# Layer ends, the first product cycle and head 17's projections of a two-layer encoder: squares in eight tiles, other orders, and readers on other engines

## The reference

```
layer 0: h = rmsnorm(x);  8 latent-attention heads + 8 differential heads  ->  x += concat(heads) @ w_out
         h = rmsnorm(x);  x += (silu(h @ w_gate) * (h @ w_up)) @ w_down            # w_gate, w_up: 1024 x 2816
layer 1: h = rmsnorm(x);  q, k, v, q_idx, k_idx, w_idx = split(h @ w_in)
         score = sum_heads(w_idx * relu(q_idx . k_idx));  keep the best keys of each query: 128 (prompt), 48 (sample)
         8 heads: softmax(q.k + bias, kept keys only) @ v   ->  x += concat(heads) @ w_out
         h = rmsnorm(x);  x += (silu(h @ w_gate) * (h @ w_up)) @ w_down
y = rmsnorm(x)
```

## Time and profile before

| | |
|---|---|
| median of 3 runs | 1752.54 us (1750.75 to 1753.04) |
| the profiled execution | 1750.98 us, span 1749.2 us |
| TensorE busy | 1683.5 us, 96% of the span |
| VectorE, ScalarE, Pool busy | 1114.9, 802.3, 598.0 us |
| mean granted clock of TensorE | 0.987 |

### The profile page before, as it was taken

One profiled execution on the slowest core, in us unless ns is written; L12 is line 12 of the kernel. 1 busy time (PEld: TensorE's weight loads), 2 busy tenths in 40 slices (PEclk: granted clock), 3 DMA queues, 4 the chain that ended last, 5 costly groups with the idle time before them and its releaser, 6 DMA issues.

```text
span 1749.2 us, 31768 instructions
## 1 busy us (share of the span) xinstructions
PE 1683.5 (96%) x12345; PEld 1622.6 (93%) x12345; DVE 1114.9 (64%) x2087; ACT 802.3 (46%) x1515; POOL 598.0 (34%) x455
## 2 busy tenths in 40 slices
PE   7999999999999899999999999799998999999998
PEld 6889998899898899999999999799988999999998
DVE  4666555645556697478477689533346974884776
ACT  4355545344546455145235444443355551452453
POOL 3344435454533322012102345464453220121022
PEclk9999999999999999999999999899999999999999
DMA  7121232322232124233323232332323232333231
GB/s 203 51 60 49 63 85 67 84 82 72 76 100 72 49 63 119 73 93 91 107 74 88 66 90 64 98 94 67 104 64 85 76 106 73 97 96 98 73 88 64
DMA packets 252105, 145.46 MB, mean 83 GB/s; under 512 B 21934, under 2 KB 242156, under 8 KB 251956
## 3 DMA queue, kind: packets, MB, share of 16 engines
q1 hardware_dynamic: 247080, 135.41, 27.3%
q0 software_dynamic: 4032, 7.77, 1.7%
q10 hardware_dynamic: 844, 0.24, 0.1%
HBM read 130.69 MB, written 15.32 MB: 83 GB/s over the span
## 4 chain that ended last, share of the span: by engine, by line
PE 82%; DVE 10%; ACT 4%; issue 2%; DMA 1%; POOL 1%; ACTq 0%; DVEq 0%; POOLq 0%
PE ACC L1191 40%; PE ACC L1551 7%; PE ACC L1553 7%; PE ACC L1552 7%; PE T L1191 3%; PE ACC L1446 2%; PE S L1191 2%; PE S L1421 2%; DVE SCO L2646 1%; DVE TOP L2643 1%; PE S L1553 1%; PE S L1551 1%; PE S L1552 1%; ACT PR L1976 1%; PE T L1434 1%
## 5 line engine op out<-in xcount | busy, mean ns | idle before, releaser
L1191 PE MATMUL ACC<-XGh,WH 128*128 128x288 f32 x1024 | 234.9, 311 | 9.2 <-DVE YK L2499 4.2
L3075 POOL TENSOR_TENSOR WL<-RAW,WH 128x1024 fp32r<-128x1024 f32 (+3 forms) x84 | 180.6, 2154 | 175.2 <-ACT WH L1851 174.8
L1191 PE MATMUL ACC<-XGl,WH 128*128 128x288 f32 x1024 | 222.1, 299 | 0.0
L1191 PE MATMUL ACC<-XGh,WL 128*128 128x288 f32 x1024 | 221.8, 299 | 0.0
L3224 POOL TENSOR_TENSOR HF<-SG,U 128x576 f32<-128x576 f32 x44 | 64.1, 1458 | 438.4 <-ACT SG L2111 411.7
L1851 ACT ACTIVATE WH<-RAW 128x1024 fp32r<-128x1024 f32 (+3 forms) x159 | 153.1, 971 | 81.9 <-PE ACC L1191 43.7
L1551 PE MATMUL ACC<-TB,WH 128*128 128x288 f32 x640 | 189.0, 295 | 0.6
L1553 PE MATMUL ACC<-TB,WL 128*128 128x288 f32 x640 | 188.8, 295 | 0.0
L1552 PE MATMUL ACC<-TB,WH 128*128 128x288 f32 x640 | 188.4, 294 | 0.0
L1191 PE MATMUL ACC<-HH,WH 128*128 128x288 f32 x1032 | 179.2, 295 | 0.0
L1191 PEld LDWEIGHTS ACC<-XGh,WH 128*128 128x128 f32 x1024 | 165.1, 192 | 15.0 <-DVE YK L2499 5.1
(11 more groups left out here) (427 smaller groups left out, 4361.6 us busy)
## 6 DMA issues: line engine op xcount, KB each, us to landing
RAW<-in_w_gate_dram SPq DMA_DIRECT2D x44, 512.0 KB, 3.9
RAW<-in_w_up_dram SPq DMA_DIRECT2D x44, 512.0 KB, 4.7
RAW<-in_w_down_dram SPq DMA_DIRECT2D x32, 512.0 KB, 4.0
RAW<-in_w_in_even_dram SPq DMA_DIRECT2D x29, 512.0 KB, 5.2
RAW<-in_w_in_odd_dram SPq DMA_DIRECT2D x28, 512.0 KB, 4.5
RAW<-in_w_out_even_dram SPq DMA_DIRECT2D x16, 512.0 KB, 4.2
RAW<-in_w_down_dram SPq DMA_DIRECT2D x16, 384.0 KB, 3.5
RAW<-in_w_out_odd_dram SPq DMA_DIRECT2D x8, 512.0 KB, 5.1
```

Of the source, the lines that this page charges most:

```text
L1191: ins = pe.matmul(out[0:m, 512 * b:512 * b + width], left, right[:, b * width:(b + 1) * width], start=(first and part == 0), stop=(last an ...
L3075: pool.tensor_tensor(WL[slot][:, 0:n], RAW[slot][:, 0:n], WH[slot][:, 0:n].bitcast(F32), ALU.subtract).then_inc(w_lo_pool, 1)
```

## The change

**Squares.** At norms 1 and 3 (the layers' attention ends) ScalarE writes the squares to eight tiles SQB and waits for nobody; VectorE adds them up in three wide additions at the start of `ffn`, in place of Pool's eight. **Output tiles.** Tile 7 of both bursts uses pair 1 and not 0. `first_half` runs the two products with MIXh first, waiting for job_hi, and the one with MIXl after it, waiting for job_lo; in layer 1 tiles 0 and 2 are begun before the weighted values of head 23, tiles 1 and 3 after them, and four tiles are halved in place of three. Head 23's last output tile is added to X before the turned probabilities of slot 5 are split.

**First cycle.** TensorE does all of u0 before the sum of squares, and three steps of g1 between the sum and its spreading. VectorE and ScalarE work the token sums, weight sums and gates in another order, and hidden_hi(0) moves up.

**Heads 16 and 17.** ScalarE reads q, k and v of head 17 from PSUM, Pool multiplies them by RSTD (y_made). ScalarE also takes KF and VF of head 16. VectorE's late selection is in one piece. Pool loads the cached keys of head 17 before head 16. Job v of head 16 is in slot 2, job k of head 17 in slot 4.

```
-    return 3 if h == 23 else 4
+    return {16: 2, 23: 3}.get(h, 4)
...
-    BURST_PAIRS = {14: (3, 0, 2, 1, 3, 0, 2, 0), 22: (1, 3, 0, 2, 1, 0, 2, 0)}
+    BURST_PAIRS = {14: (3, 0, 2, 1, 3, 0, 2, 1), 22: (1, 3, 0, 2, 1, 0, 2, 1)}
...
+            if norm in (1, 3):
+                return SQB[:, m, :]
...
+            def first_half(p, m, low):
+                out = pair(acc.at("wo", p, m)) if low else open_pair("wo", p, m)
+                wh, wl = unit_ready("wo", p, m // 4)
+                cols = slice((m % 4) * P, (m % 4 + 1) * P)
+                if low:
+                    pe.wait_ge(job_lo, jobs.made("o", p))
+                else:
+                    pe.wait_ge(job_hi, jobs.made("o", p))
+                for left in (wh,) if low else (wh, wl):
+                    for b in range(2):
+                        right = (MIXl if low else MIXh)[:, 0, b * HALF:(b + 1) * HALF]
+                        pe.matmul(out[:, 512 * b:512 * b + HALF], left[:, cols], right, start=(left is wh and not low), stop=False)
...
                     if kind_of(h) == "dsa":
-                        first_half(h - 1, 0)
+                        for low in (False, True):
+                            first_half(h - 1, 0, low)
+                            first_half(h - 1, 2, low)
...
                 plain("g", 0, 6, DT)
+                plain("u", 0, 3, DT)
                 norm_sum(norm)
-                plain("u", 0, 3, 6)
+                plain("g", 1, 0, 3)
                 norm_rows(norm)
-                plain("u", 0, 6, DT)
-                for m in range(1, PLAIN):
-                    plain("g", m, 0, DT)
-                    plain("u", m, 0, DT)
+                plain("g", 1, 3, DT)
+                plain("u", 1, 0, DT)
...
+                if kind_of(h) == "dsa":
+                    whole_first_half(3)
+                halved = 4 if kind_of(h) == "dsa" else 3
...
-                unread = n - 1 if norm == 0 else n
-                if unread > 0:
-                    act.wait_ge(sacc, unread)
+                if norm == 0 and n > 1:
+                    act.wait_ge(sacc, n - 1)
...
+                    if h == 16 and s == 1:
+                        take_first_values()
...
+            def take_projection(what):
+                before = {"q": ("v", 16), "k": ("q", 17), "v": ("k", 17)}[what]
+                dst = {"q": YQ[:, :], "k": raw_keys(17)[:, 0:NT], "v": raw_values(17)[:, 0:NT]}[what]
+                act.wait_ge(acc_done, acc.made(what, 17))
+                act.wait_ge(acc_free, acc.made(*before))
+                if what == "q":
+                    act.wait_ge(job_lo, jobs.made("q", 16))
+                act.activation(two(dst), halves(pair(acc.at(what, 17))), ACT.Copy,
+                               scale=DSA_SCALE / DIFF_SCALE if what == "q" else 1.0).then_inc(acc_free, 1)
...
+            take_projection("q")
             cached_keys_hi(16)
             begin("k", 17)
             job("q", 17)
+            take_first_keys()
             begin("v", 17)
+            take_projection("k")
+            take_projection("v")
...
-                    if s == 1:
+                    if s == 1 and h != 16:
                         take_values(h)
+                    if h == 23 and s == 5:
+                        evacuate(("wo", *out_tile(h, s)), add_to_x(out_tile(h, s)[1]))
...
+            def add_squares(norm):
+                dve.wait_ge(sq_done, XFIN * norm + DT)
+                link(dve.tensor_tensor(SQB[:, 0:4, :], SQB[:, 0:4, :], SQB[:, 4:8, :], ALU.add))
+                link(dve.tensor_tensor(SQB[:, 0:2, :], SQB[:, 0:2, :], SQB[:, 2:4, :], ALU.add))
+                dve.tensor_tensor(SACC[:, :], SQB[:, 0, :], SQB[:, 1, :], ALU.add).then_inc(sacc, XFIN)
...
                 begin("u", layer, 0)
+                evacuate(("u", layer, 0), lambda out: dve.tensor_copy(two(U[:, 0, :]), halves(out)))
                 token_sum(layer, 1)
-                evacuate(("u", layer, 0), lambda out: dve.tensor_copy(two(U[:, 0, :]), halves(out)))
+                seven_low("WG", layer, 0, PLAIN)
                 token_sum_lo(layer, 1, 1)
-                seven_low("WG", layer, 0, PLAIN)
-                token_sum(layer, 2)
                 evacuate(("g", layer, 1), times(G[:, 1, :], RSTD))
                 mix("S1", layer, 0, PLAIN)
                 mix("S2", layer, 0, PLAIN)
+                token_sum(layer, 2)
                 seven_low("S12", layer, 0, PLAIN)
+                evacuate(("u", layer, 1), lambda out: dve.tensor_copy(two(U[:, 1, :]), halves(out)))
                 mix("S3", layer, 0, PLAIN)
...
-            write_projection(17, "q")
             cached_keys_lo(16)
-            take_keys(16)
-            select_rounds(LATE_TILES, 0, 2)
-            write_projection(17, "k")
-            select_rounds(LATE_TILES, 2, 5)
-            write_projection(17, "v")
-            select_rounds(LATE_TILES, 5, 8)
+            select_rounds(LATE_TILES, 0, 8)
...
+            def scale_projection(what):
+                y = {"q": YQ[:, :], "k": raw_keys(17)[:, 0:NT], "v": raw_values(17)[:, 0:NT]}[what]
+                pool.wait_ge(acc_free, acc.made(what, 17))
+                pool.tensor_tensor(y, y, RSTD[:, :], ALU.mult).then_inc(y_made, 1)
+
             begin("q", 17)
+            scale_projection("q")
             begin("k", 17)
+            load_cached_keys(17)
             job("q", 17)
             begin("v", 17)
+            scale_projection("k")
+            scale_projection("v")
```

More of the change, by code:

```diff
@@ L297, in plan_attention @@
                 tr.add("k", x)
-            if s == 5 and h >= 16 and x is not None:
+            if s == 5 and h > 16 and x is not None:
                 jobs.add("k", x)
@@ L2021, in attention @@
                             job("k", g)
+                        if h == 16 and s == 4:
+                            job("k", x)
                         if h == 1 and s == 4:
@@ L2140, in cycle @@
                     ahead(layer, part, 1, "P5")
-                if c >= 2:
+                if c >= 2 and (before or part):
                     hidden_hi(layer, part, c - 2)
@@ L2146, in cycle @@
                     seven_copy("t1", layer, part, c)
+                    if not before and not part:
+                        seven_high("S3", layer, part, c)
                 if before:
@@ L2895, in ffn @@
                 seven_low("S3", layer, 0, PLAIN)
-                evacuate(("u", layer, 1), lambda out: dve.tensor_copy(two(U[:, 1, :]), halves(out)))
                 for part, n in enumerate(PARTS):
```

70 lines of the change are left out of this document (50 added, 20 removed).

## The result

The changed kernel takes 1738.01 us, median of 5 runs (1735.87 to 1742.06); the kernel before, in the same comparison, 1751.21 us, median of 5 (1749.23 to 1753.04). The ratio is 0.9929, 95% interval 0.9911 to 0.9948: 13.2 us faster. The forecast was 1740.5 us in a range of 1729 to 1747.

The account below looks back on a forecast made before the run. With TensorE busy 96% of the span, the prediction targeted its waits and half-rate stretches: 6.8 + 3.9 + 2.2 - 1.7 = 11.2 us, giving 1739.8 or 1741.3 by baseline. It forecast 1740.5 us, range 1729 to 1747.

Parts of the forecast that it names:

- Part A: Head 16 and the way into head 17: shorter waits and less half-rate work, 6.8 us gained, bounds 8.5 and 3.5.
- what is late next: Head 16: with the VF wait gone, tile 3's scores wait 2.6 us for SEL; 4.4 us are kept.
- The one fall of the clock: Head 16: one half-rate stretch of 3.41 us behind the new waits, costing 1.7 us.
- Part B: End of layer 0: Pool's additions gone, second cycle begins at 633.7 not 637.67; 3.9 us gained, bounds 7.4 and 0.
- Part C: End of layer 1: last tile 4.0 us earlier, second cycle at 1377.0 not 1379.24; 2.2 us gained, bounds 6 and -1.
- The further fall of the clock: Second cycle, both layers together: one more half-rate stretch behind the new waits, -1.7 us.
- The contention of the second cycle: From G to the second cycle: 1.7 us less waiting, three overlaps with Pool instead of two; 20.3 us, not 21.1.
- the rule that I weighed as an alternative: Shared port, second cycle: full blocking costs 0.6 us more per overlap, leaving 2.2 us of Part B, 0.5 of Part C.
- TensorE as the pace everywhere: Whole kernel: VectorE keeps up in cycle 2, no new wait lowers the clock; 21.4 us gained, 1729.6; chance 0.17.
- The wide additions late: Layer ends: 3 to 4 us more on VectorE's additions or contention, only Part A left; 1744; chance 0.16.
- Slower by VectorE's lateness: Both layer ends: additions moved to VectorE make it late, 8 us per layer giving 1755.8; chance 0.04.
- No change that shows: ScalarE's added work eats head 16's gain, late additions eat the layer ends'; 1750 to 1753; chance 0.07.

Follow-up runs that it names:

- ends alone: The changed kernel with heads 16 and 17 as before, so only the layer-end edits remain: 1747.31 us, ratio 0.9983.
- the pair alone: The kernel before with only tile 7 of both bursts moved to pair 1: 1751.62 us, ratio 1.0006.
- The old first-cycle order: The changed kernel with the first cycle's old order on TensorE, VectorE and ScalarE, wide additions and pairs kept: 1743.9 us, ratio 0.9959.
- Pool's squares: The changed kernel with the squares in one tile again, Pool's eight additions and ScalarE waiting for each: 1750.34 us, ratio 0.9996.
- the zeros of Pool: The changed kernel with Pool's products for feature tiles 0 and 1 replaced by zero fills, leaving those products out: 1735.75 us, ratio 0.9920.
- v whole in slot 2: The changed kernel with all eight steps of head 18's values in slot 2 while head 16 is selected: 1738.23 us, ratio 0.9926.
- heads alone: The kernel before with only the edits of heads 16 and 17: 1744.08 us, ratio 0.9958.
- Pool held back: The changed kernel with ScalarE reading u0 and u1, plus waits holding Pool's first-cycle products at three places: 1735.64 us, ratio 0.9908.

## Why the prediction was right

**Part A, 6.8 us predicted, 6.7 measured, in part by luck.** The row maxima came 2.3 us earlier and not 2.6, SEL 3.3 and not 3.6, and the wait for SEL was 2.30 us and not 2.6. Differences of this size are also between kernels with the same head 16: SEL stands 87.33, 87.56 and 87.58 us after the dots in before, ends alone and the pair alone, and 83.75 to 84.29 in the kernels that keep all of the new head. So whether KF's copy was worth the 0.60 us that I gave it can't be told: with q, k and v back on VectorE the maxima begin 72.30 us after the dots, with the old head 72.65 to 72.90. SEL gives the time of the first scores of head 17, as "what is late next" said. Of the 5.7 us up to them 3.3 come from the mask and 2.4 from what follows it, where the transfer of KC was waited for and where half-rate work lay; no run undoes the early transfer alone.

The one fall of the clock that I priced at 1.7 us was two of 3.41 us in the profiled execution, one ahead of the scores of head 17 (1.2 us, 10.81 against 9.57) and one right behind them, where before had half-rate work too. The kernel in which ScalarE reads u0 and u1 has the same head 16 and one fall there, as I priced it. From the dots to the KC of head 23 it takes 277.86 us, against 286.00 before and 279.32 in the changed kernel: 8.1 us and not 6.8. I had the gain apart from the clock some 1.3 us too small, and the second fall took about that back.

**Part B, 3.9 predicted, 4.3 measured.** Each event lies within 0.5 us of its forecast. Pool's additions are what the gain hangs on, as said: with them back it is gone. The additions of the squares and TensorE arrive together, as said (SACC is ready at 608.16, the sum begins at 608.31). The old first-cycle order shows what a wait there goes with: 3.59 us, then 6.8 us at half rate.

**Part C, 2.2 predicted, 2.2 measured** from the first addition into X, to 0.13 us at the last tile, the sum and P1; some 2.0 with the 0.2 us lost ahead of it. The wait for MIXl is 0.2 us there, the ones for X 0.48.

**The further fall of the clock, -1.7: wrong.** Behind the new waits of 2.24 and 0.56 us in cycle 2 the changed kernel's trace has none. With it taken out of the sum, my parts give 12.9 us against 13.2 measured. That is the largest part of the 2.5 us by which 1738.01 lies under the forecast. Another 0.5 is that the forecast stood on 1751.7 us for before, between two values, and the median of five runs was 1751.21. In two kernels with the same waits, ends alone and Pool's squares, the clock did fall in layer 1's second cycle, so the term was not baseless but no certainty.

**The contention of the second cycle: the right total by a wrong price.** From before's 21.1 us I took 1.7 of waits and added one overlap more, at about 0.9, which gave 20.3 against 20.45 measured. But VectorE loses no third overlap. The two of before are these rows of its timeline:

```profile
620.92 2.23 DVE L2816 TENSOR_TENSOR TB<-XD,TB 128x1152 fp32r<-128x1152 f32 x1 [0.57 <-ACT TB L2125]
...
633.96 1.25 DVE L2767 TENSOR_TENSOR WL<-RAW,WH 128x512 fp32r<-128x512 f32 x1
```

The same two take 1.35 and 0.68 us where Pool stands still, so before's overlaps cost 0.88 and 0.57 us, 1.45 together. The changed kernel's two cost 1.24 and 1.22, 2.46 together, and 2.28 us of them reach P1. The step became 1.0 us dearer through two fuller overlaps and not through a third one: that 1.0 is nearly the 0.9 that I charged is luck.

The Trainium skill's page "SBUF — State Buffer" (section "Who interferes with whom") has the rule that I weighed as an alternative: the later of two instructions is blocked until the first has finished, and this holds if VectorE's instruction reads two operands from SBUF. The rows of the two queues agree with it to 0.14 us, WL<-T,WH agrees with its exception, and the zeros of Pool, which read nothing, cost VectorE nothing. I wrote that the trace agrees with the rule's sign only, and that was wrong for before's trace too: Pool's HF, issued at 620.50, needs 1.44 us, and 1.35 behind its end is 623.29; the row of TB ends at 623.15. The mean of XGl at 1.30 us, from which I took a share of the overlap, was a mean over instructions of 0.80 to 1.97 us that met Pool at different points of its own.

**The rivals.** TensorE as the pace everywhere (1729.6): no, the waits in cycle 2 and for SEL are there. The wide additions late (1744): no as the kernel stands, but its mechanism is real, since the old order of TensorE brings it out at 1743.9. Slower by VectorE's lateness: no. No change that shows: no; ScalarE had room for it in head 16.

## What to carry to other kernels

A wait names the last thing that was late, not what made it late: taking away the 4.19 us ahead of the last tile gave nothing until VectorE, two steps back, was freed of Pool's reads. Before giving two engines work side by side, look at where the operands lie: here a sum on VectorE with both operands in SBUF and a product on Pool queued for each other, one with an operand in PSUM didn't. And when work is moved to a bound engine, as the wide additions were, find the work on the waiting engine that can be put in front of it; here the new order of the first cycle, five steps of u0 ahead of the sum in it, was worth 5.9 us.

## What was not expected of the hardware

The clock falls or does not fall behind the same wait. KC of head 23 was waited for equally long in the changed kernel and in the one with v whole in slot 2. Timeline of TensorE and the stretch behind it, the changed kernel:

```profile
1293.10 0.30 PE L1369 MATMUL T<-IDN,KC 128*128 128x128 f32 x1 [1.72 <-DMA KC<-in_cache_dsa_k_dram]
```

```profile
1294.00:1297.40 3.40, 3.40 (x17) 3.40 (x16) 1.26 (x3) 0.00 (x0) 1.57 (x2) 0.50 0.06 19
```

And the kernel with v whole in slot 2:

```profile
1288.65 0.30 PE L1369 MATMUL T<-IDN,KC 128*128 128x128 f32 x1 [1.71 <-DMA KC<-in_cache_dsa_k_dram]
```

```profile
1289.50:1292.90 3.40, 3.40 (x29) 3.34 (x28) 1.82 (x6) 0.58 (x3) 1.66 (x2) 1.00 0.06 19
```

17 matmuls against 29 in 3.4 us, some 1.7 us lost, with the same wait of 1.7 us and the same work ahead of it since head 17. In the other thirteen kernels the clock doesn't fall behind this wait. Behind the wait of 2.30 to 2.33 us for SEL it fell in five profiles and stayed in three (heads alone, ScalarE reads u0 and u1, Pool held back). Each such stretch costs what a small edit is worth; runs of one kernel here spread over 3 to 9 us. The fourteen waits of 3.10 to 5.19 us in all the profiles, those of a kernel's start apart, were each followed or accompanied by half-rate work. The Trainium skill's page "TensorE: Matmul & The Clock Gate" (section "Part 1: The HAM clock gate") says of a kernel's start that the count of slow matmuls varies from run to run; these rows show the like deep inside a kernel. What decides it behind a short wait, no run shows. To price such a fall as certain, as I did in cycle 2, is a coin thrown into a sum.
